# A two-layer pair of transformer blocks on one core: the recurrent layer's middle, done in two halves instead of straight through

## The reference

```python
def rglru_mixer(h, w_in, conv_w, conv_b, w_a, b_a, w_x, b_x, lam, w_out):
    proj = h @ w_in                                  # 1024 -> 2048
    xr, gate = proj[..., :LRU_WIDTH], proj[..., LRU_WIDTH:]
    xc = conv_b
    for j in range(CONV_WIDTH):                      # 4 taps
        xc = xc + xp[:, j:j + S] * conv_w[j]         # xp: xr, padded in front
    r = sigmoid(xblk @ w_a + b_a)                    # 8 blocks of 128 x 128
    i = sigmoid(xblk @ w_x + b_x)                    # xblk: xc in 8 blocks
    a = exp(-8 * r * softplus(-lam))
    u = sqrt(1 - a * a) * (i * xc)
    # state = a_t * state + u_t, over the 256 tokens; hs: all states
    y = hs * silu(gate)
    return y @ w_out                                 # 1024 -> 1024
```

## Time and profile before

| | before |
|---|---|
| median of 3 runs | 961.73 us (961.27 to 964.24) |
| profiled execution: its time | 962.43 us |
| profiled execution: its span | 960.6 us |
| TensorE busy | 847.3 us, 88% of the span |
| VectorE busy | 739.9 us, 77% |
| ScalarE busy | 521.8 us, 54% |
| GpSimd busy | 76.7 us, 8% |
| mean granted clock of TensorE | 0.965 of full |

### The profile page before, as it was taken

One profiled execution on the slowest core, in us unless ns is written; L12 is line 12 of the kernel. 1 busy time (PEld: TensorE's weight loads), 2 busy tenths in 40 slices (PEclk: granted clock), 3 DMA queues, 4 the chain that ended last, 5 costly groups with the idle time before them and its releaser, 6 DMA issues.

```text
span 960.6 us, 14972 instructions
## 1 busy us (share of the span) xinstructions
PE 847.3 (88%) x5749; PEld 779.3 (81%) x5749; DVE 739.9 (77%) x1153; ACT 521.8 (54%) x897; POOL 76.7 (8%) x118
## 2 busy tenths in 40 slices
PE   0487698999999999997999999999798999999946
PEld 0277577999899988996789999999678999789935
DVE  3879777888788778877778888676778857789675
ACT  0355555654444557456474345544465867664962
POOL 1000100001000000023000022010000000000200
PEclk9888899999999999999899999999889999999979
DMA  8877645677979665985746789987354775457411
GB/s 330 294 222 249 233 152 198 213 248 277 335 255 333 247 220 203 379 320 171 287 161 233 270 264 289 278 234 247 132 154 131 227 257 172 136 174 222 154 66 44
DMA packets 122678, 216.31 MB, mean 225 GB/s; under 512 B 12235, under 2 KB 97975, under 8 KB 115440
## 3 DMA queue, kind: packets, MB, share of 16 engines
q1 hardware_dynamic: 106828, 134.79, 42.2%
q0 software_dynamic: 12960, 72.46, 21.9%
q10 hardware_dynamic: 2820, 8.11, 2.4%
HBM read 214.18 MB, written 1.15 MB: 224 GB/s over the span
## 4 chain that ended last, share of the span: by engine, by line
PE 59%; DVE 22%; ACT 9%; issue 6%; DMA 3%; SPq 0%; DVEq 0%; ACTq 0%
PE bank L528 11%; PE bank L529 11%; PE bank L530 11%; PE bank L534 7%; PE bank L535 7%; PE bank L536 7%; DVE w_lo L1549 5%; DVE modsum L1579 3%; DMA raw<-in_mod_w 2%; ACT w_hi L1054 2%; ACT kk L1121 1%; DMA modraw<-in_mod_w 1%; PE bank L654 1%; PE bank L600 1%; DVE kk L2140 1%
## 5 line engine op out<-in xcount | busy, mean ns | idle before, releaser
L528 PE MATMUL bank<-h_hi,w_hi 128*128 128x256 f32 (+2 forms) x1184 | 340.6, 288 | 15.0 <-DVE h_lo L1702 8.6
L1549 DVE TENSOR_TENSOR w_lo<-raw,w_hi 128x1024 fp32r<-128x1024 f32 (+1 forms) x250 | 292.5, 1206 | 75.4 <-ACT w_hi L1054 74.9
L529 PE MATMUL bank<-h_lo,w_hi 128*128 128x256 f32 (+2 forms) x1184 | 336.3, 284 | 0.0
L530 PE MATMUL bank<-h_hi,w_lo 128*128 128x256 f32 (+2 forms) x1184 | 336.1, 284 | 0.0
L1054 ACT ACTIVATE w_hi<-raw 128x1024 fp32r<-128x1024 f32 (+1 forms) x250 | 249.2, 1028 | 80.5 <-PE bank L530 28.8
L528 PEld LDWEIGHTS bank<-h_hi,w_hi 128*128 128x128 f32 (+2 forms) x1184 | 227.4, 192 | 21.1 <-issue 17.8
L529 PEld LDWEIGHTS bank<-h_lo,w_hi 128*128 128x128 f32 (+2 forms) x1184 | 227.3, 192 | 1.3 <-issue 0.5
L530 PEld LDWEIGHTS bank<-h_hi,w_lo 128*128 128x128 f32 (+2 forms) x1184 | 227.2, 192 | 0.2
L534 PE MATMUL bank<-w_hi,o_hi 128*128 128x512 f32 x312 | 126.7, 406 | 18.4 <-DVE o_lo L2083 13.9
L535 PE MATMUL bank<-w_lo,o_hi 128*128 128x512 f32 x312 | 123.2, 395 | 0.0
L536 PE MATMUL bank<-w_hi,o_lo 128*128 128x512 f32 x312 | 123.1, 395 | 0.0
(11 more groups left out here) (274 smaller groups left out, 1157.9 us busy)
## 6 DMA issues: line engine op xcount, KB each, us to landing
raw<-in_ffn_w_in SPq DMA_DIRECT2D x88, 512.0 KB, 6.0
modraw<-in_mod_w POOLq DMA_DIRECT2D x36, 1024.0 KB, 7.0
raw<-in_ffn_w_out SPq DMA_DIRECT2D x44, 512.0 KB, 7.2
modraw<-in_ada_w POOLq DMA_DIRECT2D x16, 1024.0 KB, 5.3
raw<-in_attn_w_in SPq DMA_DIRECT2D x26, 512.0 KB, 5.5
raw<-in_moba_w_in SPq DMA_DIRECT2D x24, 512.0 KB, 8.7
modraw<-in_mod_w POOLq DMA_DIRECT2D x16, 512.0 KB, 4.4
modraw<-in_ada_w POOLq DMA_DIRECT2D x16, 512.0 KB, 5.0
```

The costliest lines, as they stand in the source:

```text
L528: pe.matmul(dst, cut(hi(u)), a_hi, start=first, stop=False, skip_group_check=True)
L529: pe.matmul(dst, cut(hi(u)), a_lo, start=False, stop=False, skip_group_check=True)
L530: return pe.matmul(dst, cut(lo(u)), a_hi, start=False, stop=last, skip_group_check=True)
L1549: dve.tensor_tensor(lo(v), raw_unit(v), hi(v).bitcast(F32), ALU.subtract).then_inc(sem("w_lo_ready"), 1)
```

## The change

The order of the weight chunks is now xr0, xr1, l_gate0, wax0, xr2, xr3, l_gate1, wax1, l_gate2, l_gate3, lru_o (before: xr0 to xr3, wax0, l_gate0, wax1, l_gate1 to l_gate3, lru_o). TensorE multiplies in that order. ScalarE and VectorE take the first half (tiles 0 to 3) up to its exponentials ahead of chunks xr2 and xr3, take its root and scans ahead of the second half's gates, and finish it up to `o_low` ahead of the second half's scans. In VectorE's list the taps of a chunk (`branch`) now stand ahead of two of the low parts and the `modulate` that stood before them, and the banks of gates and output gates are shared out anew. The number of instructions is the same, except for two more table loads on ScalarE.

```diff
     lin = w["lru_w_in_2"][0]
-    for m in range(4):
-        cols(("xr", m), lin, m * 256)
     a_and_x = [w[f"lru_w_{name}_2"][0].rearrange("n w v -> w n v") for name in ("a", "x")]
     for i in range(2):
+        for m in (2 * i, 2 * i + 1):
+            cols(("xr", m), lin, m * 256)
+        cols(("l_gate", i), lin, 1024 + i * 256)
         out.append((("wax", i), [(src[:, 4 * i:4 * i + 4], 0) for src in a_and_x], 128))
-        for m in ((0,), (1, 2, 3))[i]:
-            cols(("l_gate", m), lin, 1024 + m * 256)
+    for m in (2, 3):
+        cols(("l_gate", m), lin, 1024 + m * 256)
...
-        gate_banks = [[(4, 5), (6, 7)], [(1, 2), (3, 4)]]
-        l_gate_banks = [0, 5, 6, 2]
+        gate_banks = [[(5, 6), (7, 3)], [(1, 5), (6, 7)]]
+        l_gate_banks = [4, 0, 2, 3]
...
+            for m in (0, 1):
+                turn_chunk(("xr", m), None if m else 5)
+            columns_chunk(("l_gate", 0), bank[l_gate_banks[0]], (h_hi, h_lo))
             gates(0)
+            for m in (2, 3):
+                if m == 3:
+                    pe.wait_ge(sem("rg_read"), 8)
+                turn_chunk(("xr", m), None)
             pe.wait_ge(sem("turn_read"), turn_of[("xr", 0)] + 1)
-            columns_chunk(("l_gate", 0), bank[l_gate_banks[0]], (h_hi, h_lo))
+            columns_chunk(("l_gate", 1), bank[l_gate_banks[1]], (h_hi, h_lo))
+            pe.wait_ge(sem("turn_read"), turn_of[("xr", 1)] + 1)
+            gates(1)
             pe.wait_ge(sem("turn_read"), turn_of[("xr", 3)] + 1)
-            pe.wait_ge(sem("rg_read"), 2)
-            gates(1)
-            pe.wait_ge(sem("rg_read"), 8)
-            columns_chunk(("l_gate", 1), bank[l_gate_banks[1]], (h_hi, h_lo))
             columns_chunk(("l_gate", 2), bank[l_gate_banks[2]], (h_hi, h_lo))
+            columns_chunk(("l_gate", 3), bank[l_gate_banks[3]], (h_hi, h_lo))
             pe.wait_ge(sem("rg_read"), 16)
-            columns_chunk(("l_gate", 3), bank[l_gate_banks[3]], (h_hi, h_lo))
-            pe.wait_ge(sem("turn_read"), turn_of[("l_gate", 2)] + 1)
+            pe.wait_ge(sem("turn_read"), turn_of[("l_gate", 1)] + 1)
             out_projection("lru_o", 10)
...
+            for m in (0, 1):
+                first_taps(m)
+                branch_high(m)
+            ahead(unit0("l_gate", 0) + AHEAD)
+            gates_out(0)
+            decay(0)
+            first_taps(2)
+            branch_high(2)
+            first_taps(3)
+            input_root(0)
+            branch_high(3)
+            ahead(unit0("l_gate", 1) + AHEAD)
+            gates_out(1)
+            ahead(unit0("l_gate", 2) + AHEAD)
+            decay(1)
+            ahead(unit0("l_gate", 2) + 1 + AHEAD)
             gate_out(0)
             gate_out(1)
+            gated_high(0)
+            gated_high(1)
+            ahead(unit0("l_gate", 3) + AHEAD)
+            input_root(1)
             gate_out(2)
-            gated_high(0)
             gate_out(3)
...
+            def branch(m):
+                u = unit0("xr", m) + 1
+                ahead(u + AHEAD - 2)
+                dve.wait_ge(sem("w_used"), u + 1)
                 b = bank_of[("xr", m)]
                 for j in (2, 1, 0):
...
+            branch(0)
+            ahead(unit0("xr", 0) + 1 + AHEAD)
+            modulate(1)
+            branch(1)
+            xc_low(0)
+            ahead(unit0("xr", 1) + 1 + AHEAD)
+            modulate(1)
+            xc_low(1)
+            ahead(unit0("l_gate", 0) + AHEAD)
+            rates(0)
+            branch(2)
+            ratio(0)
+            xc_low(2)
+            ahead(unit0("xr", 2) + 1 + AHEAD)
+            branch(3)
+            xc_low(3)
+            ahead(unit0("xr", 3) + 1 + AHEAD)
+            modulate(1)
+            scans(0)
+            modulate(1)
+            ahead(unit0("l_gate", 1) + AHEAD)
+            rates(1)
+            ahead(unit0("wax", 1) + 1 + AHEAD)
+            ratio(1)
+            ahead(unit0("l_gate", 2) + AHEAD)
+            gated_rows(0)
+            gated_rows(1)
+            o_low(kk, 0, 20)
+            o_low(kk, 1, 20)
+            ahead(unit0("l_gate", 2) + 1 + AHEAD)
+            scans(1)
```

More of the change, by code:

```diff
@@ L1010, in _ @@
             norm_turns(5)
-            for m in range(4):
-                turn_chunk(("xr", m), None if m else 5)
             def gates(i):
@@ L1466, in _, with first_taps @@
             gate_bias(5)
-            for m in range(4):
+            def first_taps(m):
                 b = turned(("xr", m))
@@ L1479, in _, with branch_high @@
                         [P, D])).then_inc(sem("final_in"), 16)
+            def branch_high(m):
                 act.wait_ge(sem("xc_full"), 2 * m + 2)
@@ L1490, in decay, with gates_out @@
                 act.activation(tiles(qz, a, b), tiles(qz, a, b), ACT.Exp).then_inc(sem("decay_exp"), 1)
-            for i in range(2):
+            def gates_out(i):
                 product("wax", i)
@@ L1499, in _, with input_root @@
                                        bias=pcol[pb][:, n:n + 1]).then_inc(sem("rg_read"), 1)
-                ahead(unit0("l_gate", i) + AHEAD)
-                decay(i)
-                ahead(unit0("l_gate", i) + 1 + AHEAD)
-            for i in range(2):
+            def input_root(i):
                 act.wait_ge(sem("ratio_ready"), i + 1)
@@ L2129, in xc_low @@
                                       sem("xc_ready"), 1)
-            for m in range(4):
-                product("xr", m)
+            def branch(m):
+                u = unit0("xr", m) + 1
+                ahead(u + AHEAD - 2)
+                dve.wait_ge(sem("w_used"), u + 1)
                 b = bank_of[("xr", m)]
@@ L2148, in _, with rates @@
                 dve.nop().then_inc(sem("turn_read"), 1)
-                if m:
-                    xc_low(m - 1)
-                modulate(1)
-            xc_low(3)
-            for i in range(2):
-                a, b = 4 * i, 4 * i + 4
-                ahead(unit0("wax", i) + 1 + AHEAD)
+            def rates(i):
                 for k in range(4):
@@ L2160, in _, with ratio @@
                                       ALU.mult).then_inc(sem("rate_ready"), 1)
-                ahead(unit0("l_gate", i) + AHEAD)
+            def ratio(i):
+                a, b = 4 * i, 4 * i + 4
                 dve.wait_ge(sem("decay_exp"), 2 * i + 2)
@@ L2181, in _ @@
                                   tiles(bias, 2 * m, 2 * m + 2), ALU.mult).then_inc(sem("l_gated"), 1)
-                if m:
-                    o_low(kk, m - 1, 20)
-            o_low(kk, 3, 20)
+            branch(0)
[29 more added lines that the diff above has]
+            scans(1)
+            ahead(unit0("l_gate", 3) + AHEAD)
+            for m in (2, 3):
+                gated_rows(m)
+            for m in (2, 3):
+                o_low(kk, m, 20)
             out_projection("lru_o", lambda i: fold(10, (0, 1)) if i == 2 else None)
```

22 lines of the change are left out of this document (9 added, 13 removed).

## The result

The changed kernel takes **953.25 us** in the median of 6 runs (952.32 to 958.0), against 961.05 (959.18 to 964.24) for the kernel before beside it: ratio 0.9924, 95% interval 0.9898 to 0.995. That is 7.8 us faster, where 4.7 were predicted, and 1.35 us under the low end of the range (954.6). The profiled execution took 952.38 us.

What follows compares the result with a forecast made beforehand. The output product's start, after TensorE's 13.86 us wait for the elementwise chain, was taken as the bound. The walk put it at 922.5, 4.7 us sooner, with 33.4 us behind: 961.73 - 4.7 = 957.0 us, range 954.6 to 960.6.

Steps and rivals of the forecast that it cites:

- T: Start of the output product: forecast at 922.5, 4.7 us ahead of 927.19, with the span's end 33.4 us behind it.
- First half: Walk from the first taps to the first half's decay: gate products end at 880.0, sigmoids at 883.0, exponentials at 887.6.
- Wait 1: TensorE's wait for xc_low(1) in the first half's gate products: 1.9 us until 876.4, plus 1.4 us of clock.
- Second half's sigmoids: ScalarE waits for lru_o's first load until 905.2, then high part and table load; sigmoids end at 910.5.
- The fourth rate held by GpSimd, 1.9 us: VectorE's last second-half rate falls beside GpSimd's product and is held 1.9 us, so rates end at 913.0.
- the second rival: TensorE's product list bounds the output product's start: 921.0 to 920.1, gain 6.2 to 7.1, about 955.2 us; chance 0.20.
- TensorE's own way: TensorE's products up to the output product: l_gate3 ends at 920.1, 2.4 us of slack, no gain over 7.1 possible.
- Behind T: From the output product's start to the span's end: still 33.4 us, no new wait in later units.
- the charge is in the 33.4 already: The low-clock loss at the output product's start needs no extra charge; the 33.4 us after it include it.
- nothing opens: No new wait inside the output product: units 0 to 3 end at 935.0, unit 4 has 2.6 us of slack.
- Table loads: Two added on ScalarE, nine in place of seven after 855, 1.28 us each, without the skill's 1.38 us drain.
- all of it beside other waits: The two added table loads' 2.6 us of ScalarE time run alongside other waits.

Runs made afterwards that it cites:

- both: Changed kernel with one low part ahead of the first half's scans and, in both halves, ScalarE's load-waiting high part behind the sigmoids: 956.96 us, ratio 0.9949.
- low_ahead: Changed kernel with one low part, for the third gate chunk's second unit, ahead of the first half's scans on VectorE: 957.08 us, ratio 0.9946.
- taps_behind: Changed kernel with VectorE's postponed low parts put back ahead of each pair of convolutions: 953.93 us, ratio 0.9933.
- low_ahead_no_gpsimd: low_ahead with both gated-input products on VectorE, not GpSimd: 955.4 us, ratio 0.994.
- clock_kept: Kernel before with 36 spare products on TensorE between the fourth gate chunk and the output product: 959.31 us, ratio 0.9987.
- spare_copy: Changed kernel with one spare copy on ScalarE between the second half's exponentials and the first half's silus: 955.77 us, ratio 0.9936.
- the second one: Repeat comparison: the changed kernel as it is, timed again against the kernel before: 953.83 us, ratio 0.9926.
- straight_tail: Kernel before, its order of chunks and products kept, with only the tail split in two halves: 953.47 us, ratio 0.9925.
- no_gpsimd: Changed kernel with both gated-input products on VectorE, not GpSimd: 954.02 us, ratio 0.9922.

## Why the prediction was off

The direction and the main lever held, one step of the mechanism and the size did not: 957.0 was forecast, and 953.25 to 953.83 measured. The steps, with after's instants moved by 3.42:

- *T is the lever, and 33.4 us follow it.* Right to 1.5 us. All fourteen stages are T plus 31.9 to 34.3.
- *First half.* Wait 1 was 2.14 us (predicted 1.9), the sigmoids began at 880.5 (880.0), VectorE waited for the first taps of xr2 until 890.4 (890.1). The limit was not TensorE, though, but a load ahead of the sigmoids (1.97 us, ends 878.1), with the table load behind it. The 1.4 us of clock charged at wait 1 were not paid (1.00 in 873.4 to 876). Two errors that cancelled: that the sigmoids came out right was luck. In both, without that load ahead of them but with the low clock behind wait 1, the first sigmoids waited for TensorE's gates and began at 25.4 us of the stage, no sooner than the 25.1 of the changed kernel.
- *Second half's sigmoids.* Load waited for until 905.4 (905.2), sigmoids end 910.8 (910.5). Right.
- *The fourth rate held by GpSimd, 1.9 us.* **This is the step that failed.** Rates ended at 911.0, not 913.0, and T came at 921.25, not 922.5: 1.25 us, since ScalarE's own high part (to 911.6) was next. That is the condition of the second rival ("GpSimd does not hold the fourth rate"), and its T of 921.0. I gave it 0.20. Its 955.2 looks like what the stage gives (961.73 - 6.58 = 955.15), but that is part luck: 0.64 of the 6.58 comes from behind T, where it expected nothing, and TensorE's own way, after which it is named, was not the bound. low_ahead and taps_behind show that the hold is real where the two meet otherwise (3.22 and 3.29 us), and low_ahead_no_gpsimd prices it: 1.61 us of T.
- *TensorE's own way ends at 920.1.* It ended at 920.44, 0.81 us ahead of T. Its waits were 2.71 and 3.34 us where 0.8, 1.3 and 3.8 were listed. Right in sum, and not the bound: in low_ahead_no_gpsimd, where nothing holds the rates, TensorE is ready 2.88 us ahead of T, and T comes no sooner (66.18 against 65.85).
- *Behind T, "the charge is in the 33.4 already".* **The second miss.** The charge was in the 33.4, but it hangs on the wait at T, and with T 1.25 us sooner this was 0.81 instead of 2.4 us. clock_kept sizes it at 1.55 us. Of this 0.64 came through. Most of the rest went to unit 4, which starts 11.73 us behind T, in clock_kept 10.98. By the instants (its row names no releaser) it waited for its own low part, which stands behind `o_low` 2 and 3 and which the prediction had not listed: ready at 932.9, while TensorE came at 932.4, 2.6 us sooner than the 935.0 on which "nothing opens" rested.
- *Table loads.* Nine against seven, 1.28 us each, the next instruction 0.02 us behind (913.68 to 914.97). The Trainium skill (ScalarE: Activation LUTs, What ACT_TABLE_LOAD costs) has 2.66 us for a switch; no run here shows its drain. But the prediction's "all of it beside other waits" holds only up to the sigmoids: behind them ScalarE leads, and a load there would, I infer, be paid in full, as spare_copy's 1.15 us were.

1.25 and 0.64 make 1.9 of the 3.1 us between -4.7 and -7.8. The remaining 1.2 lie within the first comparison's interval (4.8 to 9.8 us): the second one, with 17 runs of before, gives -7.1 with 6.6 in its interval.

Where the gain comes from, the prediction had only half seen. Before, T came 21.0 us behind the second sigmoids; in the changed kernel 10.4. The sigmoids themselves came 4.7 us *later* in the stage, and straight_tail, with both halves' products straight through, gets the same total. What pays, as far as these runs separate it, is that the first half's root and scans, and the second half's, no longer stand between the exponentials and T. The interleaved chunks and the convolutions in front pay nothing.

## What to carry to other kernels

Where an output product waits for an elementwise chain, ask first what in that chain belongs to the part that it starts with; moving the rest behind it was worth 7 us here, and reordering the products in front nothing. When several orders give the same time, look for one engine's list that sums to it in each: put a spare instruction of 1 us into the suspect's list, and if the start moves by as much, move work off it. A wait that disappears can give back clock, or bring TensorE to a weight that is not ready; reckon both when something moves by a microsecond.

## What the hardware showed that I had not expected

- **Who waits, VectorE or GpSimd, is not fixed.** GpSimd's product of 2.4 us held four rates to 3.22 and 3.29 us (1.14 alone), four scans to 4.59 and 4.69 (2.44). In both executions of the changed kernel and in spare_copy it gave way instead: 5.82, 5.94 and 6.02 us, with VectorE's rates and three low parts at full speed. It began 0.72 and 0.45 us into the rates where it held them, 1.00, 0.88 and 0.78 where it waited. Beside the changed kernel's first product both were slower: 3.38 us for the product, 5.71 for three low parts of 3.49. That it gets in at some boundary between VectorE's instructions fits these, but why at one and not at the next stays open, and instants on GpSimd are rough.
- **The low clock does not follow from a wait's length alone.** Behind the same 2.14 us wait in front of the first gates the clock stayed at 1.00 in both executions of the changed kernel, and fell in low_ahead, both, spare_copy, no_gpsimd and low_ahead_no_gpsimd (0.51 over the 3.2 us behind it in the last). 1.94 us was followed by it before, though only from about 893, more than 1 us behind the wait; 1.95 in clock_kept was not; 2.96 us in low_ahead_no_gpsimd was not (1.00 from 910.4 to 914). Every wait of 3.3 us and more in these runs, twelve in all, was.
- **A high part costs VectorE 0.69 us** (128x1024 to fp32r), and ScalarE 1.04. A low part takes 1.22, so VectorE makes both parts in 1.9 us; I had reckoned 1 us for the high part.
